# A two-layer hybrid block: projection chunks in a new order, softmax heads between their token tiles, all modulation chunks in the attention, and the second norm folded into the MLP's output

## The reference

```python
hn = rms_norm(x, ln1); proj = hn @ w_in                 # 1024 -> 2824 columns
mq, mk, mv, sq, sk, sv, xqk, xv, xo, xi, xf = split(proj)
mq, mk = rope(rms_norm(heads(mq), ..)), rope(rms_norm(heads(mk), ..))
y_moba = moba_attention(mq, mk, mv)                     # 6 heads; one block of 256: causal softmax
qk = silu(causal_depthwise_conv(xqk, conv_w, conv_b))   # 4 mLSTM heads: q and k
h = mlstm(lq, lk, xv, xi + igate_b, xf + fgate_b) * sigmoid(xo)
y_mlstm = rms_norm(h, mlstm_norm)
sq, sk = rope(rms_norm(heads(sq), ..)), rope(rms_norm(heads(sk), ..))
y_swa = swa_attention(sq, sk, sv, sinks)                # 6 query heads, 2 key heads, window 128
x = x + concat(y_moba, y_mlstm, y_swa) @ w_out
u = rms_norm(x, ln2) @ w_up
x = x + square(relu(u)) @ w_down                        # 1024 -> 4096 -> 1024
```

## Time and profile before

| | |
|---|---|
| three runs | 1978.15, 1978.58, 1980.98 us |
| the profiled execution | 1976.19 us |
| its span in the trace | 1974.3 us, mean granted PE clock 0.96 |
| busy: PE, DVE, ACT, POOL | 1885.4 (95%), 1110.1 (56%), 883.3 (45%), 41.1 us (2%) |
| weights read | 339.74 MB, mean 173 GB/s |
| chain that ended last | PE 89%, DVE 6%, ACT 2%, POOL 1% |

### The profile page before, as it was taken

One profiled execution on the slowest core, in us unless ns is written; L12 is line 12 of the kernel. 1 busy time (PEld: TensorE's weight loads), 2 busy tenths in 40 slices (PEclk: granted clock), 3 DMA queues, 4 the chain that ended last, 5 costly groups with the idle time before them and its releaser, 6 DMA issues.

```text
span 1974.3 us, 26091 instructions
## 1 busy us (share of the span) xinstructions
PE 1885.4 (95%) x11138; PEld 1614.4 (82%) x11138; DVE 1110.1 (56%) x1204; ACT 883.3 (45%) x1144; POOL 41.1 (2%) x29
## 2 busy tenths in 40 slices
PE   7989999999999999899999998998999999989998
PEld 6767999787689989686899996877999886867997
DVE  4765555465465555465755645566555564665554
ACT  5445444443354445443544443435444544344442
POOL 0100000010000000000000000000000000000000
PEclk9969999996899999999999998999999998998999
DMA  7507555651575666347655553356655653373652
GB/s 244 182 13 265 187 181 187 214 171 43 177 230 190 192 197 220 129 138 235 209 188 184 188 171 107 115 205 213 191 185 180 216 167 107 107 234 117 186 189 85
DMA packets 226187, 342.48 MB, mean 173 GB/s; under 512 B 9908, under 2 KB 114712, under 8 KB 225944
## 3 DMA queue, kind: packets, MB, share of 16 engines
q1 hardware_dynamic: 224880, 339.45, 52.8%
q10 hardware_dynamic: 1192, 1.36, 0.2%
HBM read 339.74 MB, written 1.05 MB: 173 GB/s over the span
## 4 chain that ended last, share of the span: by engine, by line
PE 89%; DVE 6%; ACT 2%; issue 1%; POOL 1%; ACTq 0%; DVEq 0%; POOLq 0%
PE PS L1557 16%; PE PS L1559 15%; PE PS L1558 15%; PE PS L1573 9%; PE PS L1574 9%; PE PS L1575 9%; PE PS L1904 2%; PE PS L1528 1%; DVE LO L995 1%; PE PS L1885 1%; PE PS L1894 1%; PE PS L1593 1%; PE PS L1603 1%; POOL RS L560 1%; PE PS L1732 1%
## 5 line engine op out<-in xcount | busy, mean ns | idle before, releaser
L995 DVE TENSOR_TENSOR LO<-RAW,HI 128x2048 fp32r<-128x2048 f32 (+1 forms) x274 | 621.3, 2276 | 458.2 <-ACT HI L579 458.0
L579 ACT CAST HI<-RAW 128x2048 fp32r<-128x2048 f32 (+1 forms) x274 | 516.0, 1895 | 305.5 <-PE PS L1559 243.4
L1573 PE MATMUL PS<-AH,HI 128*128 128x256 f32 x1488 | 427.4, 287 | 0.3 <-issue 0.3
L1574 PE MATMUL PS<-AL,HI 128*128 128x256 f32 x1488 | 424.2, 285 | 0.0
L1575 PE MATMUL PS<-AH,LO 128*128 128x256 f32 x1488 | 424.1, 285 | 0.0
L1557 PE MATMUL PS<-HI,AH 128*128 128x512 f32 (+2 forms) x848 | 323.7, 382 | 5.5 <-ACT GA L925 3.5
L1558 PE MATMUL PS<-LO,AH 128*128 128x512 f32 (+2 forms) x848 | 316.1, 373 | 0.0
L1559 PE MATMUL PS<-HI,AL 128*128 128x512 f32 (+2 forms) x848 | 315.9, 373 | 0.0
L1573 PEld LDWEIGHTS PS<-AH,HI 128*128 128x128 f32 x1488 | 289.2, 194 | 2.8 <-issue 2.2
L1574 PEld LDWEIGHTS PS<-AL,HI 128*128 128x128 f32 x1488 | 289.0, 194 | 1.6 <-issue 1.0
L1575 PEld LDWEIGHTS PS<-AH,LO 128*128 128x128 f32 x1488 | 288.6, 194 | 0.0
(11 more groups left out here) (220 smaller groups left out, 1576.3 us busy)
## 6 DMA issues: line engine op xcount, KB each, us to landing
RAW<-in_w_ff SPq DMA_DIRECT2D x96, 1024.0 KB, 5.4
RAW<-in_w_in SPq DMA_DIRECT2D x80, 1024.0 KB, 5.1
RAW<-in_w_mod SPq DMA_DIRECT2D x48, 1024.0 KB, 5.1
RAW<-in_w_up SPq DMA_DIRECT2D x32, 1024.0 KB, 5.5
RAW<-in_w_down SPq DMA_DIRECT2D x32, 1024.0 KB, 5.0
RAW<-in_w_o SPq DMA_DIRECT2D x12, 1024.0 KB, 5.9
RAW<-in_w_out SPq DMA_DIRECT2D x8, 1024.0 KB, 5.0
RAW<-in_w_attn_out SPq DMA_DIRECT2D x6, 1024.0 KB, 5.1
```

The lines of the kernel that those rows point to most:

```text
L579: return nc.scalar.copy(dst, src)
L995: tt(LO[:, c % RAW_N, 0:n], RAW[:, c % RAW_N, 0:n], HI[:, NTH[c] % HL_N, 0:n].bitcast(F32), ALU.subtract).then_inc(s_lo, 1)
L1573: mm(o, wh, ah[:, j, :], start=j == 0, stop=False)
L1574: mm(o, wh, al[:, j, :], start=False, stop=False)
```

## The change

1. **Chunk order.** After columns 0 to 511 come columns 512 to 767 (c0+5), the output gate (c0+6), columns 768 to 1279 (c0+7, c0+8), columns 1280 to 1791 (c0+9, c0+10) and the mLSTM's v (c0+11). All of MoBA's q, k and v are there after c0+8.
2. **Pairs between token tiles.** Softmax heads go in pairs. The three MoBA pairs stand between single token tiles of the last three projection chunks, the window pairs follow.
3. **Modulation in the attention.** The eight modulation chunks of m_o and m_mlp stand together ahead of the output chunks and are multiplied between the window pairs and ahead of the mLSTM's output. One bank (3) takes their rows, bank 1 their columns.
4. **Second norm folded.** The MLP is fed x times the gain, not divided by its root mean square. Since relu(a u) squared is a squared times relu(u) squared for a > 0, the factor 1/mean square (VAR) is applied where the MLP's result is added. So the transposes of x start as soon as its half is there: the first half ahead of the last output chunk, the second between parts of the first two MLP chunks (`first_features`).

```diff
 class Layer:
-        self.m_mlp = Slot(self.c_o + 4, True)
-        self.c_mlp = self.m_mlp.next
+        self.m_mlp = Slot(self.m_o.next, True)
+        self.c_o = self.m_mlp.next
+        self.c_mlp = self.c_o + 4
...
 def chunks1(l):
-            for c in (0, 512, 1024):
+            yield from halves(w, l, 0)
+            for c in (512, C_LV + ML_H * DH):
+                yield tiled(w, l, 0, KT, c, 256), KT, 256
+            for c in (768, 1280):
                 yield from halves(w, l, c)
-            yield tiled(w, l, 0, KT, 1536, 256), KT, 256
-            yield from halves(w, l, C_LV)
+            yield tiled(w, l, 0, KT, C_LV, 256), KT, 256
             yield from mod_chunks(LAYERS[l].m_o)
+            yield from mod_chunks(LAYERS[l].m_mlp)
...
 # ACT, end of a layer
-                sum_squares(X, g0 + 8 + 2, L.m_mlp)
-                spare(L.m_mlp, 1)
-                high(4 * t0 + 8, lambda k: PAR[:, 16 + 8 * l + k:17 + 8 * l + k])
-                rows_out(L.m_mlp, (0, 2))
+                act.wait_ge(s_used, L.c_o + 2 + 1 + HL_N)
+                high(4 * t0 + 8, gain, steps=(0, 1))
+                ahead(L.c_o + 3)
+                act.wait_ge(s_used, L.c_o + 3 + 1 + HL_N)
+                high(4 * t0 + 10, gain, steps=(2, 3))
+                sum_squares(X, junk=QKT)
                 mlp(l, L.c_mlp, u0 + 2)
...
 # DVE
+            def inverse_variance(n, m):
+                dve.wait_ge(s_ss, n + 1)
+                stt(MS[:, 0:2], SSQ[:, 0, :], EPS, SSQ[:, 1, :], ALU.add, ALU.add).then_inc(s_ms, 1)
+                dve.wait_ge(s_rs, m + 1)
+                tt(VAR[:, :], RS[:, 0:NT], RS[:, 0:NT], ALU.mult).then_inc(s_src, 1)
...
+                        last = stt(res[:, t, cols], src[t], var[:, t:t + 1], res[:, t, cols], ALU.mult, ALU.add)
...
-                    if h in late:
-                        ahead(c0 + 12 - len(late) + late.index(h))
...
+                weigh()
+                maxima(0)
+                maxima(1)
+                probabilities(0)
+                qk_squares(1)
+                maxima(2)
+                probabilities(1)
+                qk_norm(1)
+                probabilities(2)
+                qk_sin(1)
+                qk_cos(1)
...
                 low(4 * t0 + 4)
+                split(L.c_o + 1)
+                for j in range(4):
+                    dve.wait_ge(s_mcol, g + 1)
+                    tt(MOD[..], PS[:, 1, 8 * j:8 * j + 8].., PAR[..], ALU.add).then_inc(s_modc, 1)
...
 # PE, from chunk c0 + 7 on
+                half_group(c0 + 7, 0, 0)
+                half_group(c0 + 8, 0, 1)
+                pe.wait_ge(s_lqk, l + 1)
+                # the 12 matmuls of the mLSTM scores
+                half_tile(c0 + 9, 0, 0, 0)
+                pe.wait_ge(s_mp, l + 1)
+                turn_qk(0); turn_qk(1)
+                half_tile(c0 + 9, 0, 0, 1)
+                scores(0); turn_qk(2); turn_weights(0)
+                half_tile(c0 + 10, 0, 1, 0)
+                scores(1); turn(0); turn_weights(1)
+                half_tile(c0 + 10, 0, 1, 1)
+                turn(1); scores(2); values(0); turn_weights(2)
+                tokens_out(c0 + 11, .., tiles=(0,))
+                turn(2); values(1)
+                tokens_out(c0 + 11, .., tiles=(1,))
+                values(2); modulation(0); modulation(1)
+                # mLSTM outputs; turn_qk(3); turn_qk(4); turn_qk(5)
+                scores(3); modulation(2); modulation(3); turn(3)
+                scores(4); modulation(4); values(3); turn(4)
+                scores(5); modulation(5); values(4); modulation(6)
+                turn(5); modulation(7); values(5)
+                transposes(SRC1 * l + 1, 4 * t0 + 4, YN, (0, 1))
+                # 16 matmuls: columns of the modulation, bank 1
+                transposes(SRC1 * l + 2, 4 * t0 + 6, YN, (2, 3), first=2)
+                pe.wait_ge(s_modc, L.m_o.g + 4)
+                half_group(L.c_o, 0, 0, ts=ts); half_group(L.c_o + 1, 0, 1, ts=ts)
+                half_group(L.c_o + 2, 1, 0)
+                residual_turned(g0 + 10, 4 * t0 + 8, (0, 1))
+                half_group(L.c_o + 3, 1, 1)
+                mlp(l, L.c_mlp, u0 + 2, NO_SLOT, 4 * t0 + 8, g0 + 11)
```

615 lines of the change are left out of this document (353 added, 262 removed).

## The result

| | before | after |
|---|---|---|
| median of the runs | 1979.78 us (4 runs, 1978.15 to 1983.73) | 1953.12 us (4 runs, 1949.23 to 1953.24) |
| the profiled execution | 1976.19 us | 1953.22 us |
| its span | 1974.3 us | 1951.4 us |

The ratio is 0.9867 with a 95% interval of 0.9845 to 0.989: faster by 1.1 to 1.6%.

What follows compares the result with a forecast made beforehand. PE bounds the first block, losing time to low clock in the softmax heads and a gap behind the output projection. Layer 0 -6.05, layer 1 -14.6 and clock +5.6 give -15: 1978.58 becomes 1963.6 us, range 1954 to 1979.

Steps and rivals of the forecast that it cites:

- MoBA pairs with projections: Layer 0, from 91.5: 34.2 us of PE work plus 1.2 us for single waits, ending at 126.9.
- window pairs with modulation: Six heads and six modulation chunks: 16.8 us of PE work at full clock, 1.1 us left open, ending at 144.8.
- into the output projection: Transposes and sixteen column matmuls bring PE to 150.4; then it waits for DVE to read the columns, to 154.85.
- the price of a head: PE's unit price of a softmax head: 1.85 us without waits, so 11.1 us for six heads.
- Up to c0+8: Layer 0's projection chunks: two 256-column chunks replace a pair of 512-column ones; c0+8 ends at 76.6, 0.5 later.
- Second norm: Output projection to MLP: the 9.84 us go, PE waits 1.3 us for AH and AL, second MLP chunk ends at 191.9.
- Loads: SP's loads only follow the new chunk order: costed at nothing; if late, about 5.5 us once a layer.
- A new wait on PE: Before the mLSTM scores PE waits for DVE's CV, 76.6 to 84.0, 7.4 us; later another 3.1 us, to 91.5.
- The last rival: Norm, CV and rotation 2.4 us earlier and pauses costing nothing: -25.5, 1953 us; chance 0.09 for either or both.
- The clock: Low clock after two exposed pauses a layer, before 91.5 and before 154.85: 1.4 us for each of four, +5.6.
- Layer 1's 8.6 us: Layer 1's softmax heads took 8.6 us longer than layer 0's; regained if its clock holds, making layer 1 -14.6.
- The first rival: Clock stays low in the window pairs of both layers, scores(3) to values(5): 27 us more, 1990.6 us; chance 0.12.

Runs made afterwards that it cites:

- experiment 7: The changed kernel with the second norm unfolded (squares, power, YN and transposes as before), the rest of the change kept: 1971.27 us, ratio 0.9967.
- experiment 8: The kernel before, with DVE waiting for POOL's power of the MoBA squares ahead of the split it did beside it: 1980.91 us.
- experiment 1: The changed kernel with a pair's scores head by head instead of head against head: 1952.39 us, ratio 0.9858.
- experiment 5: The changed kernel with both heads of a pair read from rows 0 to 63, the odd head's scores left out: 1952.94 us.
- experiment 6: The changed kernel with one modulation chunk between the scores of a window pair's two heads: 1966.13 us.
- experiment 9: As experiment 2, plus two of the four groups of column matmuls moved into PE's waits ahead of the values of pairs 3 and 4: 1931.06 us.
- experiment 2: The changed kernel with DVE's four modulation sums ahead of the last two low parts and the split of the second output chunk: 1939.46 us.
- experiment 12: The changed kernel with modulation chunks 2 to 7 ahead of the scores of pair 3 instead of between the window pairs: 1974.45 us.
- experiment 10: As experiment 9, plus CV early in DVE's wait for POOL and the split of c0+11 behind the weighing: 1930.58 us, ratio 0.9758.
- experiment 11: As experiment 10, with DVE's copy of the exponentials' transposes of pairs 3 and 4 ahead of the maxima of pairs 4 and 5: 1931.94 us.
- experiment 3: The changed kernel with DVE's product CV moved from behind the split of c0+11 into its wait for POOL: 1950.21 us, ratio 0.9848.

## Why the prediction missed

The walk of layer 0, each stretch as forecast and as measured:

| stretch | forecast, us | measured, us |
|---|---|---|
| to the mLSTM scores | up to 84.0 | up to 82.43 |
| scores to transposes of q and k | 7.5 | 7.38 |
| MoBA pairs with projections | 35.4 | 32.96 |
| window pairs with modulation | 17.9 | 18.59 |
| into the output projection | 10.05 | 11.08 |
| output projection | 22.9 | 25.62 |
| two MLP chunks | 14.15 | 14.18 |

It ends at 192.24, forecast 191.9, plus 2.8 us a layer for the clock that the forecast kept apart: 194.7. So layer 0 came out 2.4 us better, layer 1 by 4.2 (-16.0 against -14.6 + 2.8). Another 1.4 are chance in the second block, and 2.4 the carrying of a difference made against one execution over to a median that lay 2.4 us above it. That is the 10.5 us. That execution, 1976.19, was not "within the runs' spread": it lies below all three (1978.15 to 1980.98).

Two prices failed, and the clock's reasoning. Most of what the layers came out better is the price of a head: the MoBA pairs took 32.96 and 33.18 us against 35.4, 4.6 us for both layers. The other is the wait for POOL, 1.7 us in layer 0 by the transposes of q and k (89.81 against 91.5).

*Up to c0+8*, *Second norm* and *Loads* held: c0+8 ended some 0.5 us later than forecast, the wait for AL was 1.5 us (1.3 forecast), the two chunks took 14.18 (14.15), and PE never waited for RAW in either attention. The 9.84 us from projection to MLP did go, and experiment 7 shows the fold as the largest part of the change.

*A new wait on PE* had its place, its cause and its layers right: 5.3 us in both, against 7.4. Its size was off in one term, the 8.2 us from squares to norm, taken from the earlier trace rows, which measured 6.2 (69.05 to 75.29): POOL's power in it was held 2 us by DVE's split, an accident of the old order that the new one doesn't repeat (experiment 8). The last rival's 1953 us is the time that was measured, but by luck: of its two conditions the earlier norm came in part, 1.6 us instead of 2.4 (CV ended at 82.4, forecast 84.0), and pauses that cost nothing didn't come at all. It also wrote down the evidence against it, "DVE waited 4.06 us for POOL before, too", without asking what POOL was waiting for. The Trainium skill ("SBUF — State Buffer", section "SBUF: two separate sides") says that a DVE operation with two SBUF inputs and a GpSimd operation that reads SBUF exclude each other for their whole length, whichever starts first. The first half agrees with 6.14 against 4.17 us. The second doesn't: in the changed kernel the split started 1.4 us after POOL's power and ran beside it in 2.29 us, and the power kept its 4.17.

*MoBA pairs with projections*: the failed step is the unit price "a head 1.85 without waits". It was read from lone heads, and two heads on rows 0 to 63 and 64 to 127 share the 0.85 us of their scores (experiments 1, 5, 6). Three pairs, 2.55 us, are the 2.4 that the stretch is short of. The trace of before had the price, at the very first scores of the loop, where two heads stand one behind the other (x4):

```profile
98.28 0.50 PE L1724 MATMUL PS<-QKT 64*128 64x128 f32 x4 [1.34 <-DVE ME L1247]
98.60 0.61 PE L1725 MATMUL PS<-QKT 64*128 64x256 f32 x4
```

They end 0.93 us after the first start (98.60 + 0.61 - 98.28), like pair 0 of the changed kernel (93.89 + 0.60 - 93.57 = 0.92) and like the lone head at 125.18 (0.92).

The Trainium skill ("TensorE: Matmul & The Clock Gate", Part 3, on packing small matmuls) states that matmuls on different row groups run concurrently; the trace agrees, 0.85 against 1.50 us, and in either order of the two.

*Window pairs with modulation*: the same 2.55 us were saved there, but PE's work was 15.39 us, 1.1 more than the prices then give (16.8 - 2.55), and the waits were 3.2 us in place of 1.1, above all 1.36 us twice, when DVE does the maxima of the next pair ahead of the copy for the values. Together 0.7 us longer than forecast.

*Into the output projection*: the wait of 4.45 us for the modulation sums was 3.9, its cause as read. The rest of the stretch, 5.6 us forecast, took 7.2, because the clock fell in the columns. In layer 1 it fell later, and the stretch took 9.67 us instead of 11.08.

*The clock*: the sum, 5.6 us against some 7, was near by luck, and its reasoning wrong. I took 1.4 us for each of four pauses. The first pause of each layer cost nothing. The second place cost 2.9 us in layer 0 and 2.6 in layer 1 in the output projection (25.62 and 25.39 us against 22.77 at full clock in experiment 9), and in layer 0 another 1.6 us ahead of it: 7.2 us for columns and transposes that take 5.6 at full clock, as forecast. And it wasn't the pause that began it (experiment 2).

*Layer 1's 8.6 us* came, but they were read from one trace: experiment 8 shows layer 0 of the kernel before, but for one wait, in the same low clock. What the new order wins in the heads of a layer depends on what the clock did there before.

*The first rival*, low clock in the window pairs, didn't happen, but it stood nearer than its 0.12 suggest. Two edits of one place brought it about, at 13 us for both layers (experiment 6) and 29 (experiment 12, about half of it by the clock); the forecast had priced it at 27. The argument from the share of busy PE (94% forecast) was no measure: the changed kernel held the clock with 15.39 us of 18.59 busy, 83%, and experiment 6 lost it with 9.86 of 11.96, 82%, just ahead of the drop.

## To carry to other kernels

A unit price read from a trace holds for the neighbourhood it was read in: before it is multiplied, ask what ran beside the operation (another engine at its start, the other half of the array) and whether the new order keeps that, and look in the same trace for a place that already has the new neighbourhood. The longest wait in a table isn't the first to attack: the 5.3 us here were worth nothing, the 3.9 behind them 4.2 us in one layer and 5.5 in the other, the clock included. Small matmuls in two places between others cost less here than the same ones in one row (experiment 9). And before two runs are called equal or different, take out of the comparison what they have in common: 1.6 us of chance in unchanged code hid a gain of the same size in experiment 10.

## What the runs showed of the hardware

- The clock falls at matmuls of two columns although PE counts as busy all the time: 1.00 until 144.4, 0.55 from there to 148.6, with PE busy for 4.15 of 4.20 us. With all sixteen of them in a row (32 records) it fell in both layers of all eight profiles in which it was at 1.00 before, in layer 1 of the changed kernel only in the transposes just behind them. With eight in a row it held at 1.00 in experiments 9 to 11 and in the kernel before (at 156.33 and 190.59). Numbers between eight and sixteen weren't tried.
- With a pause of 3.9 us behind its fall the clock came back later, in all but one place: half clock lasted 10.2 us in ten of fourteen places, 13.6 in three and 6.8 in one; without the pause 6.8 and 3.4 (experiment 2, one profile). Identical code in identical order gave 10.2 and 13.6, so the length is in part chance.
- A POOL power that starts while DVE runs a subtraction of two SBUF tiles is held until that ends (6.14 us instead of 4.17); one that has started isn't (4.17 us), and doesn't hold the DVE operation back (2.29 us beside it, 1.23 for the product CV in experiment 3).
- The scores of two heads on different halves of PE's rows take as long as one head's, 0.85 us, whether their matmuls alternate or come head by head (0.86); on the same half they take 1.50 us, and with a matmul on all rows between them 0.85 each.
- Identical code of the second block took between 1292.8 and 1304.8 us in fourteen profiles, so that a change in the first block is read better from a mark inside the trace than from the total. The slices of the clock there (24 and 36 stand at 0.8 in the kernel before and the changed one) are at 0.9 in some of the profiles; what makes the clock drop there in one execution and not in another stays open.
